# Reordered step lists for the four mixer turns, and one more wait before the head scores

## The reference

```python
hn = rms_norm(h, norm1_g[l])
proj = hn @ w_in[l]
hq, hf, hi, hg, sq, sk, sv = jnp.split(proj, split_points, axis=-1)
y_hg = hgrn2_group(hq, hf, hi, hg, lb_all[l], hg_norm_g[l])
y_sw = swa_group(sq, sk, sv, positions, sw_q_norm_g[l], sw_k_norm_g[l], sw_sinks[l])
mix = jnp.concatenate([y_hg, y_sw], axis=-1).astype(h.dtype) @ w_out[l]
```

## Time and profile before

| | |
|---|---|
| time, median of 3 runs | 2563.52 us (2563.45 to 2564.37) |
| the profiled execution: span from first to last instruction | 2565.7 us |
| PE busy in the span | 2485.5 us (97%) |
| DVE, ACT, POOL busy | 1742.0, 1137.0, 889.3 us |
| mixer: turns 0 to 3 begin at about | 76.8, 285.1, 479.3, 673.5 us; the next stage at 864.4 us |

### The profile page before, as it was taken

One profiled execution on the slowest core, in us unless ns is written; L12 is line 12 of the kernel. 1 busy time (PEld: TensorE's weight loads), 2 busy tenths in 40 slices (PEclk: granted clock), 3 DMA queues, 4 the chain that ended last, 5 costly groups with the idle time before them and its releaser, 6 DMA issues.

```text
span 2565.7 us, 39348 instructions
## 1 busy us (share of the span) xinstructions
PE 2485.5 (97%) x14110; PEld 2019.4 (79%) x14110; DVE 1742.0 (68%) x3014; ACT 1137.0 (44%) x2164; POOL 889.3 (35%) x1018
## 2 busy tenths in 40 slices
PE   7999999999999899999999999999999999999999
PEld 5777778778777688777878888878888888888887
DVE  6788788688667565757576866876665454565765
ACT  5565566566455446535654222432223223323231
POOL 1432100000000363456244766476664222222222
PEclk9999999999999999999999999999999999999999
DMA  4522543543532531453153344333246753445654
GB/s 184 180 100 102 199 132 111 197 133 110 189 125 85 206 131 50 158 220 107 58 193 99 123 152 153 107 107 115 107 153 229 244 169 103 140 125 155 210 189 143
DMA packets 186546, 371.54 MB, mean 145 GB/s; under 512 B 13936, under 2 KB 79984, under 8 KB 183664
## 3 DMA queue, kind: packets, MB, share of 16 engines
q1 hardware_dynamic: 181200, 359.51, 41.6%
q10 hardware_dynamic: 5152, 9.51, 1.0%
HBM read 286.71 MB, written 79.89 MB: 143 GB/s over the span
## 4 chain that ended last, share of the span: by engine, by line
PE 56%; DVE 5%; ACT 2%; issue 2%; DMA 1%; POOL 1%; DVEq 0%; ACTq 0%; SPq 0%; POOLq 0%
PE bank L3223 8%; PE bank L3225 8%; PE bank L3227 8%; PE bank L3203 6%; PE bank L3199 6%; PE bank L3200 6%; PE bank L2137 3%; PE bank L2138 3%; PE bank L2142 3%; PE bank L2189 1%; PE bank L2168 1%; DMA raw<-w_cross 1%; PE bank L2179 1%; DMA raw<-w_mlp 1%; DVE c_normed L2054 0%
## 5 line engine op out<-in xcount | busy, mean ns | idle before, releaser
L428 POOL TENSOR_TENSOR wlo<-raw,whi 128x256 fp32r<-128x256 f32 x372 | 323.1, 900 | 1004.3 <-ACT whi L1130 551.0
L1523 PE MATMUL bank<-hi,whi 128*128 128x512 f32 x704 | 290.7, 413 | 2.7 <-ACT fg L1093 1.7
L1526 PE MATMUL bank<-lo,whi 128*128 128x512 f32 x704 | 278.0, 395 | 0.0
L3223 PE MATMUL bank<-hi,whi 128*128 128x512 f32 x896 | 275.8, 389 | 0.0
L3225 PE MATMUL bank<-lo,whi 128*128 128x512 f32 x896 | 275.8, 389 | 0.0
L3227 PE MATMUL bank<-hi,wlo 128*128 128x512 f32 x896 | 275.8, 389 | 0.0
L3014 DVE TENSOR_TENSOR lo<-h,hi 128x1024 fp32r<-128x1024 f32 x80 | 124.1, 1552 | 172.6 <-ACT hi L2778 172.6
L2709 POOL TENSOR_TENSOR wlo<-h,whi 128x256 fp32r<-128x256 f32 x160 | 128.2, 826 | 299.0 <-ACT whi L2770 299.0
L2137 PE MATMUL bank<-hi,whi 128*128 128x512 f32 x504 | 208.4, 413 | 10.8 <-DVE h L2030 6.5
L2138 PE MATMUL bank<-lo,whi 128*128 128x512 f32 x504 | 197.8, 392 | 0.0
L3223 PEld LDWEIGHTS bank<-hi,whi 128*128 128x128 f32 x896 | 168.2, 188 | 34.9
(11 more groups left out here) (401 smaller groups left out, 5586.6 us busy)
## 6 DMA issues: line engine op xcount, KB each, us to landing
h<-hidden_scratch SPq DMA_DIRECT2D x96, 512.0 KB, 4.2
raw<-w_mix SPq DMA_DIRECT2D x88, 512.0 KB, 4.1
raw<-w_cross SPq DMA_DIRECT2D x64, 512.0 KB, 3.5
raw<-w_mlp SPq DMA_DIRECT2D x64, 512.0 KB, 4.7
wlo<-mixer_lows_scratch SPq DMA_DIRECT2D x60, 512.0 KB, 3.7
hidden_scratch<-hT SPq DMA_DIRECT2D x116, 256.0 KB, 2.1
h<-w_mlp SPq DMA_DIRECT2D x112, 256.0 KB, 2.9
mixer_lows_scratch<-wlo SPq DMA_DIRECT2D x22, 512.0 KB, 2.9
```

The source lines that it names most:

```text
L428: last = pool.tensor_tensor(wlo[:, i, cols], raw[:, i, cols], whi[:, i, cols].bitcast(F32), ALU.subtract)
L1523: pe.matmul(out, w, hi[:, k, :], start=k == 0, stop=False)
L1526: pe.matmul(out, w, lo[:, k, :], start=False, stop=False)
L3223: pe.matmul(down_bank(i)[:], wh[:, cols], xh[:, i % 2, :], start=K == 0, stop=False)
```

## The change

The rows of TensorE, ScalarE and VectorE are written anew, and turns 1 and 2 get a row each (`ROW_1`, `ROW_2`). No step is added or taken away. One wait is added: the first score step of a head waits until VectorE has taken the attention scores of the tiles before (`a_s`), which had been in the same banks. Steps on SP and the start row are not changed; on GpSimd an empty row is put in for the new turn. Only the tail of one row is shown of the table; the places that matter are below.

```diff
-        "s3.3 T3 D3 p2 o3.0 c12 o3.1 o3.2 o3.3 L3 c14 u12 u13 M0 M1 u14 u15 p3 M2",
+        "o3.0 o3.1 o3.2 o3.3 u12 L3 u13 M0 M1 M2 u14 u15 p3",
...
-ROW_FIRST, ROW_0, ROW_12, ROW_3 = range(4)
-RMS = [s for s in order("PE", ROW_12) if s[0] in ("hg_total", "sw_norm")]
+ROW_FIRST, ROW_0, ROW_1, ROW_2, ROW_3 = range(5)
+RMS = [s for s in order("PE", ROW_1) if s[0] in ("hg_total", "sw_norm")]
...
-            for blk, row in enumerate((ROW_0, ROW_12, ROW_12, ROW_3)):
+            for blk, row in enumerate((ROW_0, ROW_1, ROW_2, ROW_3)):
                 turn(blk, order("ACT", row))
...
                             pe.wait_ge(a_kept.sem, a_kept.at(blk, h - 1))
                             pe.wait_ge(m_kept.sem, m_kept.at(blk, h * (NS - 1) - 1))
+                            pe.wait_ge(a_s.sem, a_s.at(blk, h * QT - 1))
                         if n >= 2:
```

More of the change, by code:

```diff
@@ L164 @@
         "w1 w2 w3 w4 w5 w6 w7 w8 w9 w10 w11 w12 w13 w14 w15 w16 w17 w18 w19 w20 w21 w22",
+        "",
         "",
@@ L199, in panel_steps @@
     yield pending
-ROW_FIRST, ROW_0, ROW_12, ROW_3 = range(4)
-RMS = [s for s in order("PE", ROW_12) if s[0] in ("hg_total", "sw_norm")]
-BEFORE_NORM = sum(s in RMS for s in list(order("PE", ROW_12))[:list(order("PE", ROW_12)).index(("norm_root", 0))])
+ROW_FIRST, ROW_0, ROW_1, ROW_2, ROW_3 = range(5)
+RMS = [s for s in order("PE", ROW_1) if s[0] in ("hg_total", "sw_norm")]
+BEFORE_NORM = sum(s in RMS for s in list(order("PE", ROW_1))[:list(order("PE", ROW_1)).index(("norm_root", 0))])
 CROSS_PANELS = [(role, b, n) for role, count in (("out", KT), ("xq", HEADS), ("xo", KT // 2))
```

## The result

The changed kernel takes **2525.43 us** (median of 4 runs, 2521.43 to 2525.87) against 2563.94 us for the kernel before in the same comparison: a ratio of 0.984, 95% interval 0.9828 to 0.9852, or 38.5 us less. Forecast were 2540 us, 2528 to 2556. The sign was right, and most of the waits went where they were meant to; the gain is 1.6 times the forecast one, the time lies 2.6 us outside the range, and a part of the gain comes from where nothing was forecast.

The account below looks back on a forecast made before the run. TensorE, busy 97% of the span, was taken as the bound; gains of 10.3 + 4.8 + 8.1 = 23.2 us off 2565.7 gave 2542.5, less 2.2 for the runs shown: 2540 us, range 2528 to 2556.

Parts of the forecast that it names:

- The step that failed: Whole mixer: no instruction added or removed but waits on one semaphore, so every engine's working time stays unchanged.
- and no more: All four mixer turns: an order without any wait could win at most 38 + 13 = 51 us, idle plus slow clock.
- Turn 0, 10.3 forecast: Mixer turn 0: 8.6 us of 14.2 us idle won, plus 1.7 us of half clock.
- Turns 1 and 2, 4.8 forecast: Mixer turns 1 and 2: each wins 1.5 us of waits and 0.9 of clock, 4.8 us for both.
- Turn 3 up to panel 16: Turn 3 before its tail: 4.9 us of waits and 1.7 of clock go, 6.6 us won.
- The tail: End of turn 3: waits of 10.6 us against 13.3, 2.7 won; net 0.8 us after M2's lost cover.
- The next stage: Stage after the mixer: M2 ahead of p3 no longer covers 1.9 us of the wait for panel 3's weights.
- The added wait: Score steps' new wait for VectorE, 12 places: 0 us taken; the last two bounded by 0 and some 4.5 us.
- the second (hardly any wait left, 2528): Rival, whole mixer: reserves not needed, clock falls once at most, another 12 us won, 2528 us; chance 0.13.
- The first: Rival, turn 0: VectorE's slowing by 22 us makes closer steps wait, so turn 0 wins nothing, 2550 us; chance 0.17.
- The third: Rival, whole mixer: VectorE's and ScalarE's pace lets waits only move elsewhere, 2560 to 2568 us; chance 0.09.
- The fourth: Rival, 12 later heads: head scores become the bound, waiting for joins or the added wait, 2576 us with 8 heads; chance 0.06.

## Why the prediction was wrong, and where it was right

**The step that failed** is the one with which the account opened: "No instruction is added or taken away but the waits on one semaphore, so the working time of every engine stays." For TensorE it doesn't stay: its work fell by 15.2 us (2.9, 4.2, 4.2 and 3.8 in the four turns). With it fell "and no more": turns 1 and 2 could win 4.7 us each by waits and clock, and won 8.9.

The larger part are edges: the new rows break the panel thirds less often and keep steps of a kind together. The trace of before held the price. Its start-to-start times at full clock are 1.81 us for a third between thirds, 1.91 ahead of an output, 1.93 to 1.95 behind most other steps and 2.25 behind `L`. With such medians, taken over the traces of all runs, for every step and its two neighbours, the new rows add up to 1.2, 3.7, 3.3 and 3.1 us less than the old ones, some 11 of the 15.2; the trace of before alone gives 10 to 13, as one fills in the neighbours that its rows don't have. The breaks of thirds are not all of it: turn 0 has 27 runs of thirds before and after.

The rest, some 4 us, belongs to the waits that went. Turn 2 of the kernel before, the third `m10.2` ahead of a wait and the third `m11.2` ahead of another third:

```profile
569.13 1.99 PE L1533 MATMUL bank<-hi,wlo 128*128 128x512 f32 x8
572.09 0.63 PE L1674 MATMUL bank<-con,s_sb 128*128 128x128 f32 x4 [0.97 <-DVE s_sb L1483]
...
576.23 1.98 PE L1533 MATMUL bank<-hi,wlo 128*128 128x512 f32 x8
578.04 0.39 PE L1523 MATMUL bank<-hi,whi 128*128 128x512 f32 x1
```

Both are entered with 2 us. Behind the second the next product starts after 1.81, inside that time; behind the first the idle time is counted only from its end at 571.12. So 0.17 us of this wait count as busy, and the view of waits doesn't have them. Over all steps that stand ahead of a wait these remainders are 6.6 us in the old rows and 2.6 in the new ones. I compared busy times turn by turn and never the busy time of one and the same step in two surroundings.

Without that term the account is near: waits and clock were to bring 25.1 us ahead of the loss at the next stage (18.2 + 6.9), and brought 28.5 (23.5 + 5.0). By its steps:

- *Turn 0, 10.3 forecast.* Idle time fell by 6.8 us (8.6 forecast). The waits at `D1`, at `L` (but for 0.3 us) and at `c6` went as said; of the pairs, `u3` and `u10` wait 0.7 each and `u11` 1.4. Not foreseen was ScalarE's `G2`, which holds the copy `u6` and costs 2.8. The clock cost 1.6 us more instead of 1.7 less, within what one row does from one execution to the next.
- *Turns 1 and 2, 4.8 forecast.* 17.8. All waits went (6.1 against 3.0) and all of the slow clock (3.3 against 1.8); 8.4 are work.
- *Turn 3 up to panel 16.* No wait over 0.1 us is left at `s1.0` or anywhere before `u11`: 4.9 us, as forecast, and no half clock.
- *The tail.* `c12` waits 3.5 us for the state (4.7 taken, between 3.4 and 6), `c14` 1.2 (1.2), and there are four waits of 0.7 (four forecast). The 1.9 us for `u12`, `L3`, `u13` and `u14` did not come. That such a `c12` is the weak place of the change isn't borne out: neither the outputs put first nor the spread `u` steps made the tail shorter.
- *The next stage.* Panel 3 waits 1.7 us for its weights; some 2 were forecast. But counting the move of `M2` as a loss was half the story: it covers `u14` for as much.
- *The added wait.* Nothing, as forecast.

Of the rivals, the second (hardly any wait left, 2528) came nearest in time and is not what happened: 14.8 us of waits are left. The first, that turn 0 gives its gain back since GpSimd slows VectorE, is half true: VectorE was again busy for 176.7 us in that turn and 153.7 in the next (175.2 and 154.4 before, in the turns cut exactly), and what was freed at `u7` came back at later steps. It didn't eat the gain of the turn, which is 8.1 us. The third, that the waits only move, didn't come: 38.3 us of idle time became 14.8. The fourth didn't come: only one score step waits for its joins, 0.6 us.

## What to carry to other kernels

A list of waits is not the whole price of an order. Where an engine is busy nearly all the time, measure one and the same step in different surroundings, start to start: here a break in a run of large products cost TensorE some 0.36 us where it could be read by itself, and fewer changes between steps were worth some 11 us, about half as much as the 23.5 us of idle time removed. A wait costs more than its listed idle time, too. And move the rows of engines that feed each other together: one regrouped alone was 33 us slower.

## What was not expected of the hardware

The edges: 0.36 and 0.37 us for a run of thirds more or less between outputs, with TensorE counted busy throughout. And the clock: after the same wait of 2.77 us at the same place the granted clock was 0.66 over 10 us in one execution and 1.00 in another, which makes a single profile of this kernel uncertain by some 3 us.
